# The turn between two expert passes and the last norm: rest rows packed on 128 partitions, the third slab split ahead of the output copies, one of each token's two rows gathered in the last pass, the root by Sqrt

## The chip, the cores and the metric

The kernel runs on one core of one Trainium2 chip. The metric is the device time of one execution in microseconds (us). TensorE (PE in the rows; PEld is its weight load), VectorE (DVE), ScalarE (ACT), GpSimd (POOL) and SyncE (SP) run their own instruction streams and meet at semaphores. Transfers are issued from the queues of SP, ACT and POOL.

## The reference

Two decoder layers over 512 prompt tokens and 8 sample tokens (520 rows of 1024, fp32). Each layer mixes tokens (mLSTM, gated linear attention and pooling in parallel, merged by gates) and then mixes channels: layer 0 by a dense SwiGLU, layer 1 by a mixture of eight experts of which each token uses two. A norm of each row ends the kernel. What matters here:

```python
def moe_swiglu(h, router_w, wg, wu, wd):
    ...
    top_p, top_i = lax.top_k(probs, TOP_K)
    top_p = top_p / jnp.sum(top_p, axis=-1, keepdims=True)
    ...
    for e in range(N_EXPERTS):
        out = out + comb[..., e:e + 1] * swiglu(h, wg[e], wu[e], wd[e]).astype(jnp.float32)
    return out.astype(h.dtype)
...
def rmsnorm(x, g):
    xf = x.astype(jnp.float32)
    y = xf * lax.rsqrt(jnp.mean(xf * xf, axis=-1, keepdims=True) + EPS)
    return (y * g.astype(jnp.float32)).astype(x.dtype)
```

## The kernel before

Every weight tile is a slab of 512 KB (128 partitions of 1024 fp32). SyncE loads it into one of `RAW` = 4 places of `raw`; ScalarE copies it, rounded, to `w_hi` (`split_hi`, L685 in the profile); VectorE (`split_lo`, L1025) or GpSimd (`rest`, L643) writes the remainder to `w_lo`; TensorE multiplies with both. `w_hi` and `w_lo` have `SPL` = 3 places, so a split waits until TensorE is through with the slab three before it (`slab_done`). Which slabs GpSimd takes is fixed by `REST_ON_GPSIMD`: slabs 2 and 3 of a pass and its eleven down slabs.

The experts run in passes. The router sorts the 520 x 2 chosen rows by expert into a DRAM tensor, `token_slots`, `CAP` = 160 slots for a pass; each expert has at least one pass, and in the profiled execution there are eight. A pass has `S_JOB` = 33 slabs: a gate and an up slab for each of `FE_TILES` = 11 hidden tiles, and a down slab for each; the down product of tile f runs after gate and up of tile f + 1. So slabs 0 to 3 are gate, up, gate, up, and slab 4 is the first down. The loop over the passes runs on all five engines.

While pass j multiplies, GpSimd loads the 160 rows of pass j + 1 into `rows_in` (`load_rows`): 128 rows on 128 partitions, and the other `REST` = 32 on 32 partitions. Near the end of pass j TensorE turns these rows, features to partitions, in two halves (`gather`, L1827 for the 128 and L1828 for the 32 rows): the second half of the features after the last up slab, the first half right ahead of the last down. ScalarE and VectorE split each half into `hg` (`gathered_hi`, L918; `gathered_lo`, L1376). The last down also needs `ma_parts` of the last hidden tile, which VectorE completes at L1503, in its order behind the second half of `hg`.

The turn, once the last down is done: ScalarE copies the pass's outputs from PSUM (`yt`, L960, L962), splits slab 2 of the next pass, waits for VectorE to add two partial sums of the 32 rows (L1497), issues the two stores (L966, L967), goes back to the loop's head, reloads the table for Sigmoid (L941), and takes gate tile 0 (L948) and the split of slab 3. The slabs 0 and 1 were split before. GpSimd takes the remainder of slab 2, issues `load_rows` and takes that of slab 3.

After the last pass, GpSimd waits for the stores to land (`all_stored`) and gathers both rows of each token, five tiles of tokens (four of 128, one of 8), into `first` and `second` by indirect DMA (L674), ten transfers in turn. `last_norm` then takes tile by tile: VectorE adds both rows with their shares to `xt` (L1514, L1518), ScalarE squares and sums (L974), takes Ln and Exp for the inverse root (L977, L980) and scales (L983), TensorE turns the tile back (L1956), VectorE multiplies by the gain (L1524), SyncE stores it. VectorE takes the two additions of tile i ahead of the multiplication of tile i - 1.

## Time and profile before

| | us |
|---|---|
| median of three runs | 2482.98 (2480.99 to 2484.28) |
| the profiled execution, its own time | 2478.01 |
| span of its trace | 2476.3 |
| outside the span | 1.7 |

The trace is of a single execution whose time lies 4.97 us under the median of the runs. The passes fill the trace from about 1784 us to 2431 us; the rest behind them is the last norm. In the rows, a start is counted from the first instruction; "xN" counts instructions that are shown as one; what stands in square brackets is how long the engine had been idle, and what released it.

### The profile page before, as it was taken

What the parts mean: (1) busy time and instruction counts of PE and PEld (TensorE: products, weight loads), DVE (VectorE), ACT (ScalarE), POOL (GpSimd) and SP (SyncE); (2) the same over time, 40 slices, a digit from 0 to 9 for tenths busy, and PEclk for the clock granted to TensorE, in tenths of its full rate; (3) what the DMA queues carried; (4) which work ended last, traced back from release to release, by engine and by line L of the source; (5) the groups of instructions that cost most, each with busy time, mean ns of one, the idle gap of its engine ahead of it and who ended that gap; (6) DMA issues with size and microseconds to landing.
All of it is one profiled execution on the core that took longest, in us unless ns stands there. A gap on an engine that the chain in (4) does not pass through costs nothing.

```text
span 2476.3 us, 39023 instructions
## 1 busy us (share of the span) xinstructions
PE 2235.2 (90%) x15763; PEld 2044.0 (83%) x15763; DVE 1227.6 (50%) x1718; ACT 941.7 (38%) x1258; POOL 441.4 (18%) x387
## 2 busy tenths in 40 slices
PE   6999999749899999989999997598699999999994
PEld 6999887539899999989998875398588888887883
DVE  3225433655343332232254336553377777677775
ACT  3224333141333322132244231413355555555556
POOL 0000212131000000000002121310233443444343
PEclk9999999769999999999999997699699999999996
DMA  4323422325523332323234223251377777776775
GB/s 141 93 86 99 148 75 84 111 87 167 228 79 91 93 94 86 92 64 93 86 99 148 79 79 117 86 164 60 123 223 236 225 230 227 235 233 225 236 226 173
DMA packets 102634, 341.70 MB, mean 138 GB/s; under 512 B 13128, under 2 KB 17256, under 8 KB 102248
## 3 DMA queue, kind: packets, MB, share of 16 engines
q1 hardware_dynamic: 85416, 278.46, 36.3%
q0 software_dynamic: 15568, 56.34, 6.8%
q10 hardware_dynamic: 1536, 5.24, 0.6%
q8 instruction: 89, 1.46, 0.2%
q14 instruction: 25, 0.20, 0.0%
HBM read 294.28 MB, written 46.17 MB: 137 GB/s over the span
## 4 chain that ended last, share of the span: by engine, by line
PE 61%; issue 18%; POOL 10%; DVE 5%; ACT 4%; DMA 1%; POOLq 0%; SPq 0%; ACTq 0%; DVEq 0%
PE ps L1574 49%; PE ps L1568 9%; POOL w_lo L643 9%; DVE h_lo L1045 1%; DVE sq L1040 1%; POOL br_lo L612 0%; DMA ifb<-if_bias 0%; POOL token_slots L658 0%; ACT mixed L851 0%; ACT L805 0%; ACT wgt L805 0%; DVE Cs L1262 0%; DVE num L1267 0%; DVE Cq L1264 0%; ACT w_hi L685 0%
## 5 line engine op out<-in xcount | busy, mean ns | idle before, releaser
L685 ACT ACTIVATE w_hi<-raw 128x1024 fp32r<-128x1024 f32 x488 | 514.0, 1055 | 569.3 <-PE ps L1574 492.6
L1025 DVE TENSOR_TENSOR w_lo<-raw,w_hi 128x1024 fp32r<-128x1024 f32 x383 | 473.1, 1235 | 380.9 <-ACT w_hi L685 377.5
L1574 PE MATMUL ps<-h_hi,w_hi 128*128 128x260 f32 x2800 | 587.8, 292 | 34.2 <-DVE h_lo L1045 26.0
L1574 PE MATMUL ps<-h_hi,w_lo 128*128 128x260 f32 x2800 | 573.5, 287 | 0.0
L1574 PE MATMUL ps<-h_lo,w_hi 128*128 128x260 f32 x2800 | 572.9, 287 | 0.0
L1574 PEld LDWEIGHTS ps<-h_hi,w_hi 128*128 128x128 f32 x2800 | 442.4, 193 | 56.1 <-issue 46.9
L1574 PEld LDWEIGHTS ps<-h_hi,w_lo 128*128 128x128 f32 x2800 | 441.5, 193 | 0.0
L1574 PEld LDWEIGHTS ps<-h_lo,w_hi 128*128 128x128 f32 x2800 | 440.9, 193 | 0.0
L1883 PE MATMUL ps<-hg,w_hi 128*128 128x320 f32 x1408 | 378.1, 351 | 27.7 <-POOL w_lo L643 25.4
L1885 PE MATMUL ps<-hg,w_lo 128*128 128x160 f32 x1408 | 337.3, 240 | 0.0
L643 POOL TENSOR_TENSOR w_lo<-raw,w_hi 128x1024 fp32r<-128x1024 f32 x105 | 250.2, 2387 | 397.2 <-ACT w_hi L685 397.0
L1883 PEld LDWEIGHTS ps<-hg,w_hi 128*128 128x128 f32 x1408 | 269.4, 191 | 39.1 <-POOL w_lo L643 28.0
L1885 PEld LDWEIGHTS ps<-hg,w_lo 128*128 128x128 f32 x1408 | 273.9, 195 | 3.2
L1897 PE MATMUL ps<-w_hi,ma_parts 128*128 128x512 f32 x352 | 117.4, 415 | 7.0 <-POOL w_lo L643 6.6
L1574 PE MATMUL ps<-br_hi,w_hi 128*128 128x260 f32 x384 | 81.0, 294 | 45.3 <-issue 35.9
L1482 DVE TENSOR_TENSOR ma<-gsum,msig 128x160 f32<-128x160 f32 x88 | 82.4, 936 | 52.6 <-ACT msig L948 52.6
L1574 PEld LDWEIGHTS ps<-br_hi,w_hi 128*128 128x128 f32 x384 | 62.4, 198 | 46.4 <-issue 36.7
L563 POOL DMA_DIRECT2D S_p<-S x2 | 1.2, 598 | 481.5 <-DVE S L1116 481.5
L1480 DVE TENSOR_REDUCE gsum<-ps 128x160 f32<-128x320 f32 x88 | 43.2, 490 | 85.4 <-PE ps L1885 85.2
L560 POOL DMA_DIRECT2D m_s<-ml_m x2 | 1.1, 552 | 450.3 <-DVE x L1368 450.3
L1574 PE MATMUL ps<-br_lo,w_hi 128*128 128x260 f32 x384 | 80.3, 291 | 0.0
L1574 PE MATMUL ps<-br_hi,w_lo 128*128 128x260 f32 x384 | 79.8, 290 | 0.0
(336 smaller groups left out, 2724.6 us busy)
## 6 DMA issues: line engine op xcount, KB each, us to landing
raw<-slabs SPq DMA_DIRECT2D x489, 512.0 KB, 3.9
gates_kept<-sq SPq DMA_DIRECT2D x64, 260.0 KB, 2.1
gs<-gates_kept POOLq DMA_DIRECT2D x64, 260.0 KB, 3.2
token_slots<-zeros POOLq DMA_DIRECT2D x1, 9600.0 KB, 34.7
rows_in<-token_slots POOLq DMA_DIRECT2D x9, 512.0 KB, 5.6
Cs<-ml_C POOLq DMA_DIRECT2D x8, 512.0 KB, 4.1
C_s<-Cs POOLq DMA_DIRECT2D x8, 512.0 KB, 2.9
token_slots<-yt ACTq DMA_DIRECT2D x8, 512.0 KB, 2.7
```

The costliest lines, as they stand in the source:

```text
L643: nc.gpsimd.tensor_tensor(w_lo[:, n % SPL], raw[:, place(n)], w_hi[:, n % SPL].bitcast(F32), ALU.subtract).then_inc(lo_ready_gpsimd, 1)
L685: nc.scalar.activation(w_hi[:, n % SPL], raw[:, place(n)], ACT.Copy).then_inc(hi_ready, 1)
L1025: tt_op(w_lo[:, n % SPL], raw[:, place(n)], w_hi[:, n % SPL].bitcast(F32), ALU.subtract).then_inc(lo_ready, 1)
L1040: stt_op(to, x[:, kk], gain[:, kk:kk + 1], rs[:, 0], ALU.mult, ALU.mult).then_inc(normed, 1)
L1045: tt_op(h_lo[:, kk - 1], own, h_hi[:, kk - 1].bitcast(F32), ALU.subtract).then_inc(h_lo_ready, 1)
L1480: nc.vector.tensor_reduce(gsum[:], addends(b), AX.X, ALU.add).then_inc(m_sum, 1)
L1482: tt_op(ma[:, f % 2], gsum[:], msig[:], ALU.mult).then_inc(m_gate, 1)
L1568: return mm(out, a, b, start=start, stop=stop, skip_group_check=True)
L1574: ins = mm(out[:, hf], wgt_part[:, slot, tile], in_part[:, kk, HALF * hf:HALF * (hf + 1)], start=first and not ends and in_part is in_hi, ...
L1883: mm(out[:, 0:2 * CAP], w_hi[:, (s0 + s) % SPL, kk], hg[:, kk], start=kk == 0, stop=False, skip_group_check=True)
L1885: ins = mm(out[:, 0:CAP], w_lo[:, (s0 + s) % SPL, kk], hg[:, kk, 0:CAP], start=False, stop=kk == KT - 1, skip_group_check=True)
L1897: mm(ps[:, 4 + hf_], parts[:, at:at + P], w[:, slot_n, 4 * hf_:4 * hf_ + 4], start=f == 0 and a == 0, stop=f == FE_TILES - 1 and a == 2)
```

## The change

Five edits go together.

- The 32 rest rows of a pass are no longer loaded on 32 partitions but as four quarters of their features, one below the other, on 128 partitions (`rest_in`, four transfers instead of one). TensorE turns them with two full transposes, in the second half of the features, in place of eight narrow ones spread over both halves. ScalarE and VectorE split them by an operation of their own.
- In the turn, ScalarE splits slab 2 of the next pass ahead of the two output copies instead of behind them.
- The two slots of a token are sorted (`order`), and the shares with them. The row of the lower slot lies in an earlier pass than that of the higher. GpSimd's last pass is taken out of its loop, and between its remainders it gathers the five tiles of lower rows; after the last pass only the five of higher rows are gathered.
- The inverse root of the last norm is Sqrt on ScalarE and a reciprocal on VectorE instead of Ln and Exp.
- The last norm's order: VectorE adds all lower rows first, then the higher rows tile by tile, with the gain of tile i - 2 behind the addition of tile i; ScalarE squares tile i ahead of scaling tile i - 1.

```diff
@@ GpSimd
         def load_rows(first):
-            pool.dma_start(rows_in[:, 0], slots[bass.ds(first, P)]).then_inc(rows_loaded, 16)
-            pool.dma_start(rows_in[0:REST, 1], slots[bass.ds(first + P, REST)]).then_inc(rows_loaded, 16)
+            pool.dma_start(rows_in[:], slots[bass.ds(first, P)]).then_inc(rows_loaded, 16)
+            for b in range(4):
+                pool.dma_start(rest_in[REST * b:REST * (b + 1)],
+                               slots[bass.ds(first + P, REST), D // 4 * b:D // 4 * (b + 1)]).then_inc(
+                                   rows_loaded, 16)
...
-        with pool.Fori(0, passes_pool) as j:
+        with pool.Fori(0, last) as j:
             pool.wait_ge(gathered, j * 2 + 2)
             load_rows(j * CAP + CAP)
-            for i in REST_ON_GPSIMD[1:] + [S_JOB + 2]:
-                rest(MOE0 + i, j)
+            pass_rests(j, REST_ON_GPSIMD[1:] + [S_JOB + 2])
+        pool.wait_ge(gathered, last * 2 + 2)
+        load_rows(last * CAP + CAP)
+        pass_rests(last, REST_ON_GPSIMD[1:4])
+        pool.wait_ge(y_stored, last * 32 + 1)
+        for i in range(5):
+            rest(MOE0 + REST_ON_GPSIMD[4 + i], last)
+            rows_back(first, 0, i, first_in)
+        pass_rests(last, REST_ON_GPSIMD[9:] + [S_JOB + 2])
         pool.wait_ge(all_stored, 1)
         for i in range(5):
-            rws = slice(0, tile_rows(i))
-            for k, (to, landed) in enumerate(((first, first_in), (second, second_in))):
-                pool.indirect_dma_start(to[rws, i], None, slots,
...
+            rows_back(second, 1, i, second_in)
@@ ScalarE
             nc.scalar.activation(hg_part(b, 0), gathered_ps(b), ACT.Copy).then_inc(hg_hi_ready, 1)
+            if b:
+                nc.scalar.activation(hg_rest(0), gathered_rest(), ACT.Copy).then_inc(hg_hi_ready, 1)
...
             gathered_hi(j + 1, 0)
+            split_hi(s0 + 2, j + 1)
             act.wait_ge(slab_done, j * S_JOB + (s0 + S_JOB))
...
-            split_hi(s0 + 2, j + 1)
             act.wait_ge(y_added, j + 2)
@@ VectorE
             tt_op(hg_part(b, 1), gathered_ps(b), hg_part(b, 0).bitcast(F32),
                   ALU.subtract).then_inc(hg_lo_ready, 1)
+            if b:
+                tt_op(hg_rest(1), gathered_rest(), hg_rest(0).bitcast(F32),
+                      ALU.subtract).then_inc(hg_lo_ready, 1)
...
+            inc(tt_op(order_f[:, 0], index_f[:, 0], index_f[:, 1], ALU.min))
+            inc(tt_op(order_f[:, 1], index_f[:, 0], index_f[:, 1], ALU.max))
...
+            for i in range(7):
                 if i < 5:
...
                     dve.wait_ge(second_in[i], 16)
...
+                if 1 <= i < 6:
+                    rws = slice(0, tile_rows(i - 1))
+                    dve.wait_ge(fin_root, i)
+                    nc.vector.reciprocal(rst[rws, i - 1:i], rst[rws, i - 1:i]).then_inc(fin_rs, 1)
+                if i > 1:
+                    rws = tile_rows(i - 2)
+                    dve.wait_ge(fin_turned, i - 1)
@@ TensorE
         def gather(p, b):
-            pe.wait_ge(rows_loaded, p * 32 + 32)
+            if b:
+                pe.wait_ge(rows_loaded, p * 80 + 80)
+                for c in range(2):
+                    nc.tensor.transpose(ps[:, 2 + c, P:2 * P], rest_in[:, c * P:(c + 1) * P], ident)
             for m in range(4 * b, 4 * b + 4):
-                out = ps[:, m // 2, 256 * (m % 2):256 * (m % 2) + CAP]
-                nc.tensor.transpose(out[:, 0:P], rows_in[:, 0, m * P:(m + 1) * P], ident)
-                ins = nc.tensor.transpose(out[:, P:CAP], rows_in[0:REST, 1, m * P:(m + 1) * P],
-                                          ident[0:REST, 0:REST])
+                ins = nc.tensor.transpose(ps[:, m // 2, 256 * (m % 2):256 * (m % 2) + P],
+                                          rows_in[:, m * P:(m + 1) * P], ident)
```

On ScalarE, at the end of a pass, these rows stand from the split of the first half of `hg` to the stores. First the kernel before:

```order
L918 ACTIVATE hg<-ps 128x4x160 [waits gathered]
L958 REGISTER_ALU
L959 ISA [waits slab_done]
L960 ACTIVATE yt<-ps 128x1024 [waits y_stored]
L962 ACTIVATE yt<-ps 32x1024
L682 ISA
L684 ISA [waits arrived3]
L685 ACTIVATE w_hi<-raw 128x1024 [waits slab_done]
L965 REGISTER_ALU
L966 ISA [waits y_added]
L966 DMA token_slots<-yt 128x1024
```

And the same stretch of ScalarE in the changed kernel, whose line numbers differ (L716 is the split, L994 and L996 the copies):

```order
L949 ACTIVATE hg<-ps 128x4x128 [waits gathered]
L713 ISA
L715 ISA [waits arrived3]
L716 ACTIVATE w_hi<-raw 128x1024 [waits slab_done]
L992 REGISTER_ALU
L993 ISA [waits slab_done]
L994 ACTIVATE yt<-ps 128x1024 [waits y_stored]
L996 ACTIVATE yt<-ps 32x1024
L998 REGISTER_ALU
L999 ISA [waits y_added]
L999 DMA token_slots<-yt 128x1024
```

The split of slab 2 has moved from behind the two copies to ahead of them; the wait for `y_added` still stands behind all three.

On VectorE, near the end of a pass, the changed kernel has these rows between the multiplication of the last hidden tile (L1535) and the remainder of that tile (L1551), which the last down waits for:

```order
L1535 TENSOR_TENSOR ma<-ma,usum 128x160 [waits m_up]
L1057 REGISTER_ALU
L1058 TENSOR_TENSOR w_lo<-raw,w_hi 128x1024 [waits hi_ready]
L1408 ISA
L1409 TENSOR_TENSOR hg<-ps,hg 128x4x128 [waits hg_hi_ready]
L1412 TENSOR_TENSOR hg<-ps,hg 128x2x4x32
L1551 TENSOR_TENSOR ma_parts<-ma,ma_parts 128x128 [waits m_hi]
L1551 TENSOR_TENSOR ma_parts<-ma,ma_parts 128x32
```

Before, one operation of 128x4x160 stood where L1409 and L1412 stand now; the rest is as it was.

On ScalarE the last norm of the changed kernel begins with these rows:

```order
L1044 ACT_TABLE_LOAD
L1044 ACTIVATE msig<-con 1x1 [waits y_stored]
L1008 ACTIVATE rows_in,ssq<-xt 128x1024 [waits both_added]
L1011 ACTIVATE rst<-ssq,con 128x1 [waits fin_sq]
L1008 ACTIVATE rows_in,ssq<-xt 128x1024 [waits both_added]
L1011 ACTIVATE rst<-ssq,con 128x1 [waits fin_sq]
L1016 ACTIVATE xt<-xt,rst 128x1024 [waits fin_rs]
L1008 ACTIVATE rows_in,ssq<-xt 128x1024 [waits both_added]
```

The nine table loads that stood between the Ln and the Exp of the tiles are gone; the one ahead of the wait for the stores is left.

## Rows read from the trace of the kernel before

**Rows 1.** Waits of TensorE over all passes: total us, times, longest.
```profile
PE ps L1883 <- POOL w_lo L643: 25.4, 14, 2.3
```

**Rows 2.** Windows from turn to turn: length, engines' busy us, granted clock, DMA share.
```profile
1945.75:2026.52 80.77, 76.76 (x480) 67.26 (x480) 58.32 (x89) 45.62 (x61) 32.04 (x15) 0.98 0.73 231
2026.52:2107.34 80.82, 75.96 (x480) 65.98 (x480) 58.82 (x89) 45.73 (x61) 32.04 (x15) 1.00 0.74 230
```

**Rows 3.** Timeline of TensorE, first turn: start, us, engine, line, operation.
```profile
1870.12 0.41 PE L1883 MATMUL ps<-hg,w_hi 128*128 128x320 f32 x1 [1.38 <-POOL w_lo L643]
...
1874.74 0.41 PE L1883 MATMUL ps<-hg,w_hi 128*128 128x320 f32 x1 [2.32 <-POOL w_lo L643]
```

**Rows 4.** Timeline of ScalarE, first turn.
```profile
1864.77 1.03 ACT L960 ACTIVATE yt<-ps 128x1024 f32<-128x1024 f32 x1 [1.88 <-PE ps L1901]
1865.69 1.00 ACT L962 ACTIVATE yt<-ps 32x1024 f32<-32x1024 f32 x1
1866.59 1.04 ACT L685 ACTIVATE w_hi<-raw 128x1024 fp32r<-128x1024 f32 x1
...
1869.44 1.28 ACT L941 ACT_TABLE_LOAD   x1 [1.81 <-issue]
...
1871.21 1.04 ACT L685 ACTIVATE w_hi<-raw 128x1024 fp32r<-128x1024 f32 x1
```

**Rows 5.** Timeline of VectorE, first turn.
```profile
1860.63 0.81 DVE L1376 TENSOR_TENSOR hg<-ps,hg 128x640 fp32r<-128x640 f32 x1
1861.37 0.38 DVE L1503 TENSOR_TENSOR ma_parts<-ma,ma_parts 128x128 fp32r<-128x128 f32 x2
...
1866.72 1.21 DVE L1497 TENSOR_TENSOR yt<-yt,ps 32x1024 f32<-32x1024 f32 x1 [2.94 <-ACT yt L962]
```

**Rows 6.** Timeline of GpSimd, first turn: the remainder of slab 3.
```profile
1872.34 2.34 POOL L643 TENSOR_TENSOR w_lo<-raw,w_hi 128x1024 fp32r<-128x1024 f32 x1 [1.25 <-ACT w_hi L685]
```

**Rows 7.** Timeline behind the last pass: gathers, first additions, one tile turned.
```profile
2438.08 1.00 POOL L674 DMA_INDIRECT first<-token_slots,index  x1 [1.68 <-ACT msig L1011]
...
2442.34 1.28 DVE L1514 SCALAR_TENSOR_TENSOR xt<-first,share,xt 128x1024 f32<-128x1024 f32 x1 [8.06 <-DMA first<-token_slots,index]
...
2443.94 1.28 DVE L1518 SCALAR_TENSOR_TENSOR xt<-second,share,xt 128x1024 f32<-128x1024 f32 x1 [0.31 <-DMA second<-token_slots,index]
...
2466.18 1.97 PE L1956 MATMUL ps<-con,xt 128*128 128x128 f32 x8 [3.38 <-ACT xt L983]
```

**Rows 8.** Timeline of TensorE: last transposes ahead of the last down, first turn.
```profile
1861.63 0.33 PE L1827 MATMUL ps<-con,rows_in 128*128 128x128 f32 x1
...
1862.07 0.72 PE L1897 MATMUL ps<-w_hi,ma_parts 128*128 128x512 f32 x2
```

**Rows 9.** Timeline of TensorE in the routing: sixteen full transposes in a row.
```profile
1744.74 1.97 PE L1836 MATMUL ps<-con,hf 128*128 128x128 f32 x16
```

**Rows 10.** Timelines of GpSimd and TensorE ahead of the first pass.
```profile
1772.42 0.57 POOL L650 DMA_DIRECT2D rows_in<-token_slots  x1
...
1777.16 0.45 PE L1827 MATMUL ps<-con,rows_in 128*128 128x128 f32 x1 [9.40 <-DMA rows_in<-token_slots]
...
1784.03 0.63 PE L1883 MATMUL ps<-hg,w_hi 128*128 128x320 f32 x1 [1.65 <-DVE hg L1376]
```

**Rows 11.** Lines of 2431.1 to 2477 us: count, busy us, mean ns, idle before.
```profile
L980 ACT ACT_TABLE_LOAD x5 | 6.4, 1283 | 0.1
...
L983 ACT ACTIVATE xt<-xt,rst 128x1024 f32<-128x1024 f32 (+1 forms) x5 | 5.7, 1147 | 0.2
...
L974 ACT ACTIVATE rows_in<-xt 128x1024 f32<-128x1024 f32 (+1 forms) x5 | 5.3, 1051 | 8.5 <-DVE xt L1518 8.5
L977 ACT ACT_TABLE_LOAD x4 | 5.1, 1283 | 0.1
...
L977 ACT ACTIVATE rst<-ssq,con 128x1 f32<-128x1 f32 (+1 forms) x5 | 1.5, 295 | 0.1
```

**Rows 12.** DMA issues: transfers, KB of each, median us to landing.
```profile
y_out<-x SPq DMA_DIRECT2D x4, 512.0 KB, 3.6
```

More of the change, by code:

```diff
@@ L304, in decoder @@
     xt = sb("xt", [P, 5, D], where=moe)
-    rows_in = sb("rows_in", [P, 2, D], where=moe)
+    rows_in = sb("rows_in", [P, D], where=moe)
+    rest_in = sb("rest_in", [P, D // 4], where=moe)
     yt = sb("yt", [P, 2, D], where=moe)
@@ L322, in decoder @@
     index = sb("index", [P, 2, 5], mybir.dt.int32, where=moe)
+    order_f = sb("order_f", [P, 2, 5], where=moe)
+    order = sb("order", [P, 2, 5], mybir.dt.int32, where=moe)
+    is_low = sb("is_low", [P, 2, 2, 5], where=moe)
     share = sb("share", [P, 2, 5], where=moe)
@@ L663, in _, with pass_rests, rows_back @@
         pool.wait_ge(rt.sem, rt.after("tables"))
-        passes_pool = pool.value_load(jt[:, NJ:NJ + 1], min_val=E, max_val=PASSES)
-        with pool.Fori(0, passes_pool) as j:
+        last = pool.value_load(jt[:, NJ + 1:NJ + 2], min_val=E - 1, max_val=PASSES - 1)
+        def pass_rests(j, which):
+            for i in which:
+                rest(MOE0 + i, j)
+        def rows_back(to, k, i, landed):
+            rws = slice(0, tile_rows(i))
+            pool.indirect_dma_start(to[rws, i], None, slots,
+                                    bass.IndirectOffsetOnAxis(ap=order[rws, k, i:i + 1], axis=0)).then_inc(
+                                        landed[i], 16)
+        with pool.Fori(0, last) as j:
             pool.wait_ge(gathered, j * 2 + 2)
             load_rows(j * CAP + CAP)
-            for i in REST_ON_GPSIMD[1:] + [S_JOB + 2]:
-                rest(MOE0 + i, j)
+            pass_rests(j, REST_ON_GPSIMD[1:] + [S_JOB + 2])
[7 more added lines that the diff above has]
+        pass_rests(last, REST_ON_GPSIMD[9:] + [S_JOB + 2])
         pool.wait_ge(all_stored, 1)
         for i in range(5):
-            rws = slice(0, tile_rows(i))
-            for k, (to, landed) in enumerate(((first, first_in), (second, second_in))):
-                pool.indirect_dma_start(to[rws, i], None, slots,
-                                        bass.IndirectOffsetOnAxis(ap=index[rws, k, i:i + 1], axis=0)).then_inc(
-                                            landed[i], 16)
+            rows_back(second, 1, i, second_in)
     @block.scalar
@@ L1440, in routing @@
             inc(nc.vector.tensor_copy(jt[:, NJ:NJ + 1], ends[0:1, E - 1:E]))
+            inc(ts_op(jt[:, NJ + 1:NJ + 2], ends[0:1, E - 1:E], -1.0, None, ALU.add))
             at("tables")
@@ L1466, in shares @@
             at("share")
+            inc(tt_op(order_f[:, 0], index_f[:, 0], index_f[:, 1], ALU.min))
+            inc(tt_op(order_f[:, 1], index_f[:, 0], index_f[:, 1], ALU.max))
+            for a in range(2):
+                inc(tt_op(is_low[:, 0, a], index_f[:, a], index_f[:, 1 - a], ALU.is_lt))
+                inc(tt_op(is_low[:, 1, a], index_f[:, a], index_f[:, 1 - a], ALU.is_ge))
+            at("masks")
+            inc(nc.vector.tensor_copy(order[:], order_f[:]))
+            inc(tt_op(is_low[:], is_low[:], share[:].unsqueeze(1).to_broadcast([P, 2, 2, 5]), ALU.mult))
+            at("parts")
+            inc(tt_op(share[:], is_low[:, :, 0], is_low[:, :, 1], ALU.add))
+            at("ordered")
         def addends(b):
```

78 lines of the change are left out of this document (40 added, 38 removed).

## The prediction

> **What bounds the kernel now.** I looked first at what TensorE waits for over the passes. One wait stands out: 25.4 us in 14 waits for GpSimd's remainder of a slab [rows 1]; from turn to turn, TensorE is otherwise busy, 76 of some 81 us [rows 2]. The timeline of the first turn shows that these are two waits in each of the seven turns, 1.38 us at slab 2 and 2.32 us at slab 3 [rows 3]; seven times their sum is 25.9, so nearly all of the group is there. The reader is to see that both lie behind ScalarE. Counted from the start of the output copy (1864.77), the second copy starts at 0.92, the split of slab 2 at 1.82, the table load at 4.67 and the split of slab 3 at 6.44 [rows 4]; VectorE's addition of the 32 rows runs from 1.95 to 3.16 [rows 5]; GpSimd takes slab 3's remainder at 7.57 for 2.34 [rows 6], and TensorE goes on at 9.97 [rows 3]. Every step follows on the one before it, and the split of slab 2 lies beside VectorE's addition, for which ScalarE has to wait anyway.
>
> Behind the last pass it is another chain: ten gathers issued one after the other, then five tiles through ScalarE. The gathers start at 2438.08 [rows 7], the span ends at 2476.3, so 38.2 us.
>
> **The third slab ahead of the copies.** In the changed turn, ScalarE splits slab 2 at 0 instead of 1.82, GpSimd takes the remainder from 1.1 to 3.5 (2.34 as in [rows 6]), and TensorE, which came to slab 2 at 3.97 (1870.12 less its wait of 1.38, from 1864.77) [rows 3], does not wait: 1.38 us less. But the copies now start at about 0.95 (a split takes 1.04 and the next operation of a row starts just ahead of its end, as 0.92 behind 1.03 [rows 4]), and VectorE's addition, the stores, the table load and the split of slab 3 all move back by 0.95. Before, the split cost nothing because the addition (1.21) hid it; ahead of the copies nothing hides it. Slab 3 is ready at 10.92 instead of 9.97. TensorE needs slab 3 right behind slab 2, so its 1.38 us are lost again there: it waits once, about 4.7 us, and leaves the turn **0.95 us later**. Bounds: 1.1 (the whole split, 1.04, and the step to the next engine) and 0.8 (if the last down comes 0.15 sooner, below). Seven turns: **+6.7** (5.6 to 7.7). The same 0.95 stands ahead of the stores behind the last pass; I count it there.
>
> **The packed rest rows.** A full transpose and a narrow one take 0.44 between them (1861.63 to 1862.07) [rows 8], eight such pairs a pass 3.5 us. Full transposes in a row take 1.97 / 16 = 0.12 each [rows 9]; ten take 1.2. TensorE has 2.3 us less to do in each pass. What is it worth? In the turn, the last down starts at 1862.07, as soon as the transposes end [rows 8], but VectorE has given it the remainder of the last hidden tile only at 1861.75 (1861.37 and 0.38) [rows 5]: not over 0.3 can be gained. And ahead of that remainder VectorE now has two subtractions of 512 and 256 elements for one of 640; from 0.81 for 640 and 1.21 for 1024 [rows 5] an operation costs about 0.14 and 1.04 ns an element, so the second operation adds some 0.25 with its 128 elements more. I take the two as equal: **0** at the turns, and a new wait of about 2 us ahead of the last down. Bounds: a gain of 0.3 and a loss of 0.25 a pass.
>
> Ahead of the first pass nothing covers the transposes. There the rows landed at 1777.16 and the first product started at 1784.03, 6.87 us later [rows 10]. TensorE runs there at its lower clock (a transpose is 0.45 long, against 0.33 at the turn [rows 8]), where eight full transposes take 1.97 [rows 7], twice what they take in [rows 9], 0.25 each: ten take 2.5 in place of eight pairs. Then the splits set the end: six transposes (1.5) and ScalarE's two copies (about 1.0) put VectorE's three subtractions (0.67, 0.41, 0.67 by the costs above) from 2.5 to 4.3, a gain of 2.6. Against it stand three more issues on GpSimd's queue at 0.59 each [rows 10], 1.8 if the last landing moves by all of it, 0 if it is the 512 KB of the first that end last. The first transfer has most of the bytes, so I take 0.3. **-2.3** (-0.8 to -2.6). In the passes the rows have a whole pass to land, and GpSimd is through with the issues (five at 0.6 behind slab 2's remainder, to about 6.5) before slab 3's split ends at 8.4: 0.
>
> **Lower rows in the last pass.** Five gathers of 512 KB at most, between remainders which take 2.34 and come with every down slab, 80.8 / 11 = 7.3 us apart: GpSimd has room for a 1.0 us issue [rows 7]. Their bytes run beside the slabs' at a DMA share of 0.73 [rows 2]. Gathers alone land 1.60 apart (2442.34 and 2443.94) [rows 7], so each could hold up a slab by 1.6, five 8 us; none if the share that is free takes them. **+0.3** (0 to 8), near nothing, since the free quarter of a 7.3 us step is 1.8. The sorting of slots adds some ten small operations of VectorE while it waits for the first rows anyway.
>
> **The last norm.** Per tile, the Ln, Exp and two table loads become one root: nine loads of 1.283 [rows 11], 11.5 us, go. I follow the new order from the start S of the first of five gathers. Its row tile lands at S + 4.3, the others 1.6 apart [rows 7]. VectorE has added all lower rows by then (five of 1.28 [rows 7], from the end of its last addition on). Tile 1 is added by 7.2, squared (1.05 and the reading of the sum, 1.18 together) and rooted (0.3, as the Ln [rows 11]) by 8.7; tile 0 is scaled (1.15) by 9.9 and turned (1.97 [rows 7]) by 11.9. VectorE stands at the gain of tile 0 until then, and only after it (1.2, as 1024 elements from PSUM in [rows 5]) adds tile 3, by 14.4. So tile 3 is rooted at 15.9, tile 2 scaled by 17.0, turned by 19.1; tile 3 is scaled by 19.8, behind tile 4's root, turned by 21.8, and out of VectorE by 23.0. Its store takes 3.6 [rows 12]: end at S + 26.8, 11.4 less than 38.2. S itself moves by 0.95 against the last down. **-10.4** (-9 to -12, an operation of 1.2 us either way).
>
> **Sum.** -2.3 + 6.7 + 0 + 0.3 - 10.4 = -5.7 us on the profiled execution: 2478.0 to 2472.3. The three runs lie higher, median 2482.98, a factor 1.002, so 2477.3.
>
> **Rivals.** 0.2%, about what a measurement of this kernel can tell from no change, is 5.0 us.
>
> (a) *The split is hidden after all*: slab 3 comes no later, if something other than the chain through the copies held ScalarE's table load. For it speaks that the idle time ahead of that load is put down to issuing [rows 4]; against it that the stores just ahead need VectorE's addition. The turns then cost 0: 2470.6.
>
> (b) *The transposes count*: if the last down could start 2.3 us earlier in eight passes, 18.4 less: 2459. Against it is the remainder of the last hidden tile [rows 5].
>
> (c) *The gathers collide with the slabs* at the full price, 1.6 for each of four large ones, 6.4 more: 2483.4, no change. For it: a slab's load and a gather take the same engines; against: the free share, which is as large as a gather.
>
> (d) *The clock* (slower than before). TensorE's one wait of 4.7 us replaces two of 1.4 and 2.3. After waits the granted clock has fallen: one turn's period shows 0.98 on average, so 0.04 x 80.77 = 3.2 us at the lower level of 1.2 GHz, the next shows 1.00 [rows 2]. If a longer wait brings one such spell more to each turn, TensorE loses half of it, 1.6, seven times 11.4: 2488.7. It decides from 1.5 us lost in a turn, where the gain of 5.7 turns into a loss of 5. The Trainium skill ("TensorE: Matmul & The Clock Gate", "HAM oscillation — how this bites in real kernels") speaks against this change: a wait that is long enough costs the clock, and it should be broken up. The trace agrees that the clock falls after such waits. But it also shows that the period with a spell, 80.77, is no longer than that without one, 80.82 [rows 2], since the slabs behind slab 3 wait for GpSimd anyway; by the rows the price is near 0, by the page's rule 11.4 us.
>
> (e) *Slab 2 still waits*, because its split waits for the same last down as before: it can't start ahead of it. That is so, and is in the sum; if its data had not landed by then it would lose more, but it was split without a wait for data behind the copies [rows 4].
>
> **How the numbers follow.** The sum as it stands has 0.57, and reaches from 2473.5 to 2481.5 for the bounds of the turns, the start and the last norm together; (a) 0.13, (b) 0.06, (c) 0.12, (d) 0.08; 0.04 are left for what I don't see. Under 2478.0 lie somewhat over half of the sum's case (0.33), (a) and (b), and none of the others: faster 0.52. No change: the rest of the sum's case 0.24, most of (c) 0.10, a little of the unseen 0.02: 0.36. Slower: (d), and bits of (c) and the unseen: 0.12. The range 2470 to 2486 leaves out (b), (d) and the unseen; the likeliest case's own is 2473.5 to 2481.5.
>
> **What would show it.** Right: at the turns one wait of TensorE for GpSimd of 4.5 to 5 us at slab 3 and none at slab 2; a new wait of about 2 us for `ma_parts` ahead of the last down; turn to turn 81.8 us instead of 80.8; the first product 2 us sooner; no table load between the tiles; from the first gather behind the last pass to the end some 27 us. Wrong: a period of 80.8 or less (then (a) or (b)), waits for slabs in the last pass that the passes before it lack (c), the lower clock for longer behind each turn and a period over 83 (d), or a last norm that takes over 30 us because a gather lands later than 1.6 behind the one before.

## The result

The changed kernel takes 2486.93 us (median of 12 runs, 2479.20 to 2493.31), the kernel before, run beside it, 2481.34 (12 runs, 2479.64 to 2486.76). The ratio is 1.002, with a 95% interval of 1.0011 to 1.0029: some 5 us slower, where 5.7 us faster was forecast. The profiled execution of the changed kernel took 2483.66, 5.65 more than that of before.

The waits of TensorE over all passes answer to [rows 1] (total us, times, longest):

```profile
PE ps L1938 <- POOL w_lo L655: 32.2, 7, 4.8
PE ps L1952 <- DVE ma_parts L1551: 13.7, 8, 1.7
```

So there are seven waits at slab 3 and none at slab 2, and in each pass a new one of 1.71 us for `ma_parts` ahead of the last down. In the first turn ScalarE does what was forecast, beside [rows 4]:

```profile
1864.00 1.06 ACT L716 ACTIVATE w_hi<-raw 128x1024 fp32r<-128x1024 f32 x1 [2.27 <-PE ps L1956]
1864.97 1.01 ACT L994 ACTIVATE yt<-ps 128x1024 f32<-128x1024 f32 x1
1865.87 0.99 ACT L996 ACTIVATE yt<-ps 32x1024 f32<-32x1024 f32 x1
...
1869.63 1.28 ACT L974 ACT_TABLE_LOAD   x1 [2.76 <-issue]
...
1871.40 1.04 ACT L716 ACTIVATE w_hi<-raw 128x1024 fp32r<-128x1024 f32 x1
```

From the end of the last down (1863.96 here, 1864.65 before) the split of slab 3 starts at 7.44 instead of 6.56. TensorE resumes at 10.96 instead of 10.09 (1874.92 here), 0.87 later, against a forecast of 0.95. The periods, from the end of one last down to the end of the next, are another matter. Their windows, after (length, busy us of PE, PEld, DVE, ACT, POOL, granted clock, DMA share and GB/s), answer to [rows 2]:

```profile
1863.96:1947.33 83.37, 76.11 (x475) 67.51 (x474) 58.51 (x90) 45.86 (x62) 33.53 (x18) 0.96 0.71 224
1947.33:2030.93 83.60, 76.67 (x473) 67.78 (x473) 58.26 (x90) 45.81 (x62) 33.54 (x18) 0.94 0.71 227
...
2280.14:2361.87 81.73, 75.02 (x474) 66.82 (x474) 58.45 (x90) 45.64 (x62) 33.52 (x18) 0.97 0.70 222
2361.87:2445.20 83.33, 76.22 (x473) 67.06 (x471) 58.65 (x90) 45.65 (x62) 38.33 (x23) 0.96 0.75 246
```

One period of seven, 81.73, is the forecast 81.8; the others are 82.8 to 83.6, with the clock at 0.94 to 0.96. All seven sum to 581.2 us against 566.4 before: 14.9 more instead of 6.7. The clock is lost in spells, stretches at half of it. Shorter windows show two of them (same columns), the first over a last down, the second behind a turn:

```profile
2028.20:2031.60 3.40, 3.40 (x11) 2.41 (x10) 0.66 (x2) 0.63 (x1) 0.00 (x0) 0.51 0.93 349
...
1874.60:1881.40 6.80, 6.48 (x22) 5.88 (x23) 5.74 (x8) 2.68 (x4) 2.64 (x2) 0.50 0.53 171
```

Half the clock is the level of 1.2 GHz. Here is the end of the third pass, the first with a spell over its last down: VectorE's subtraction of the second half of `hg`, then TensorE:

```profile
2025.81 0.68 DVE L1409 TENSOR_TENSOR hg<-ps,hg 128x512 fp32r<-128x512 f32 x1
...
2027.18 0.73 PE L1952 MATMUL ps<-w_hi,ma_parts 128*128 128x512 f32 x2 [1.71 <-DVE ma_parts L1551]
2027.75 0.62 PE L1952 MATMUL ps<-w_lo,ma_parts 128*128 128x512 f32 x2
2028.21 1.02 PE L1952 MATMUL ps<-w_hi,ma_parts 128*128 128x512 f32 x2
2029.02 1.06 PE L1956 MATMUL ps<-w_hi,ma_parts 128*64 128x512 f32 x2
2029.88 1.06 PE L1956 MATMUL ps<-w_lo,ma_parts 128*64 128x512 f32 x2
```

From that subtraction to the last down it is 1.37 us, against 1.44 before (1860.63 to 1862.07 in [rows 5] and [rows 8]), so the wait itself makes the last down no later. But about one microsecond behind the wait a pair of products grows from 0.62 to 1.06 us, and this last down takes 3.8 us instead of 2.6 (the four with a spell take 3.8 to 4.1). In the trace of before, five of seven turns have one half-clock spell of 3.41 us, starting 9.9 to 11.6 us behind the last down, and no last down has one. After, four turns have 6.83 us (starting at 8.9 to 10.7), three 3.41, and four last downs have 3.41 us each. Sorted by that, the periods are: 3.41 behind the turn alone, 81.73; 6.83 alone, 82.78 and 83.37; 3.41 and a spell at the last down, 83.11 and 83.33; 6.83 and a spell at the last down, 83.32 and 83.60.

The start, beside [rows 10]: TensorE's first transpose and first product.

```profile
1778.95 0.66 PE L1881 MATMUL ps<-con,rest_in 128*128 128x128 f32 x2 [12.68 <-DMA rest_in<-token_slots]
...
1783.09 0.63 PE L1938 MATMUL ps<-hg,w_hi 128*128 128x320 f32 x1 [1.76 <-DVE hg L1409]
```

The first row transfer was issued at 1773.79, so this is 9.30 us against 12.20 before (1771.82 to 1784.03): 2.9 less. But this execution came to that transfer 1.97 later, in a part of the program that the change leaves as it was.

Behind the last pass, beside [rows 7] and [rows 11]:

```profile
2453.36 1.62 POOL L689 DMA_INDIRECT second<-token_slots,order  x1 [4.65 <-ACT msig L1044]
...
2458.70 1.29 DVE L1568 SCALAR_TENSOR_TENSOR xt<-second,share,xt 128x1024 f32<-128x1024 f32 x1 [3.38 <-DMA second<-token_slots,order]
2460.61 1.28 DVE L1568 SCALAR_TENSOR_TENSOR xt<-second,share,xt 128x1024 f32<-128x1024 f32 x1 [0.62 <-DMA second<-token_slots,order]
```

No table is loaded between the tiles, and from the first gather to the end of the span it is 28.57 us (forecast 26.8); from the last down to the end 36.7, against 45.3 before: 8.6 less.

The two traces differ by 2.0 (ahead of the first transfer) - 2.9 (start) + 0.3 (first pass) + 14.9 (seven periods) - 8.6 (behind the passes) = 5.7.

### The profile page after: what moved, and what is told of

It reads as the page before. It is cut to its first block, busy times and chain, and to the rows that moved or that the text cites. A ratio compares the mean times of both kernels' runs of the same rounds, so it can differ in the third digit from the quotient of the medians.

```text
span 2481.9 us, 39000 instructions
## 1 busy us (share of the span) xinstructions
PE 2226.7 (90%) x15709; PEld 2042.6 (82%) x15709; DVE 1227.9 (49%) x1742; ACT 929.2 (37%) x1253; POOL 454.9 (18%) x414
## 4 chain that ended last, share of the span: by engine, by line
PE 61%; issue 18%; POOL 11%; DVE 5%; ACT 4%; DMA 1%; POOLq 0%; SPq 0%; ACTq 0%; DVEq 0%
PE ps L1628 49%; PE ps L1622 9%; POOL w_lo L655 8%; DVE h_lo L1078 1%; DVE sq L1073 1%; POOL rest_in L663 1%; POOL br_lo L624 0%; PE ps L1938 0%; DMA ifb<-if_bias 0%; PE ps L1952 0%; POOL token_slots L673 0%; ACT w_hi L716 0%; ACT mixed L882 0%; ACT L836 0%; ACT wgt L836 0%
## 5 line engine op out<-in xcount | busy, mean ns | idle before, releaser
L716 ACT ACTIVATE w_hi<-raw 128x1024 fp32r<-128x1024 f32 x488 | 514.6, 1055 | 596.4 <-PE ps L1628 493.4
L1938 PE MATMUL ps<-hg,w_hi 128*128 128x320 f32 x1408 | 384.6, 355 | 34.0 <-POOL w_lo L655 32.2
L1628 PEld LDWEIGHTS ps<-br_hi,w_hi 128*128 128x128 f32 x384 | 62.7, 200 | 45.3 <-issue 36.7
L1952 PEld LDWEIGHTS ps<-w_hi,ma_parts 128*128 128x128 f32 x352 | 61.6, 195 | 34.0 <-DVE ma_parts L1551 15.6
L1628 PE MATMUL ps<-br_lo,w_hi 128*128 128x260 f32 x384 | 80.9, 293 | 0.0
```

The costliest lines, as they stand in the source:

```text
L716: nc.scalar.activation(w_hi[:, n % SPL], raw[:, place(n)], ACT.Copy).then_inc(hi_ready, 1)
L1628: ins = mm(out[:, hf], wgt_part[:, slot, tile], in_part[:, kk, HALF * hf:HALF * (hf + 1)], start=first and not ends and in_part is in_hi, ...
L1938: mm(out[:, 0:2 * CAP], w_hi[:, (s0 + s) % SPL, kk], hg[:, kk], start=kk == 0, stop=False, skip_group_check=True)
L1952: mm(ps[:, 4 + hf_], parts[:, at:at + P], w[:, slot_n, 4 * hf_:4 * hf_ + 4], start=f == 0 and a == 0, stop=f == FE_TILES - 1 and a == 2)
```

## The experiments

Two theories. **The clock**: both waits that the change lengthens or opens, 4.7 us at slab 3 and 1.71 us ahead of the last down, bring longer spells at 1.2 GHz, and these make the passes longer. **The work**: the passes are longer for what runs late in them (slab 3, five row transfers, gathers), and the clock only follows. Each run below was timed in five rounds beside the kernel before; the changed kernel's ratio for comparison is 1.002. Differences between two runs are taken from their ratios.

**Filling the wait ahead of the last down.** The changed kernel, with the four transposes there (of the 128 rows; the rest rows are turned in the other half) done five times over:

```diff
-            for m in range(4 * b, 4 * b + 4):
+            for m in list(range(4 * b, 4 * b + 4)) * (1 if b or isinstance(p, int) else 5):
```

> The changed kernel, but the four transposes of the packed rest rows ahead of the last down are done five times over (same values to the same place), so that TensorE works some 1.75 us where it waited 1.71 us for the packed rows; no result changes. If the wait is what brings the half-clock spell at the last down (four passes of eight in the profile, 1.3 to 1.55 us each): those spells go, the last down takes 2.58 us in every pass, and the time falls by 4 to 6 us against the changed kernel, to 2481 to 2483. If the lower clock only follows from something else, the time stays or rises by up to 8 x 0.1 us, and the spells stay.

2476.53 us, ratio 0.9982 (0.9973 to 0.9991): 0.38% or 9.4 us below the changed kernel, more than expected. One last down, with no wait left ahead of it (the first row is the last ten of twenty transposes):

```profile
2024.33 1.25 PE L1883 MATMUL ps<-con,rows_in 128*128 128x128 f32 x10
2025.55 0.73 PE L1952 MATMUL ps<-w_hi,ma_parts 128*128 128x512 f32 x2
2026.12 0.63 PE L1952 MATMUL ps<-w_lo,ma_parts 128*128 128x512 f32 x2
2026.58 0.62 PE L1952 MATMUL ps<-w_hi,ma_parts 128*128 128x512 f32 x2
```

No last down has a half-clock spell any more. Every turn has one of 6.83 us, and its price depends on where it falls, as this kernel's windows show, the first with a spell from 10.4 us behind the last down, the second from 9.1, the third from 8.1:

```profile
1862.47:1945.64 83.17, 77.69 (x490) 69.20 (x490) 58.44 (x90) 45.86 (x62) 33.53 (x18) 0.96 0.73 225
1945.64:2028.12 82.48, 77.12 (x491) 68.84 (x490) 58.46 (x90) 45.76 (x62) 33.56 (x18) 0.96 0.72 225
...
2274.34:2356.26 81.92, 76.64 (x490) 68.46 (x490) 58.25 (x90) 45.99 (x62) 33.57 (x18) 0.96 0.72 227
```

The earlier the spell begins, the more of it lies in the wait for slab 3 (until 10.9), and the less it costs: from the third window to the first the period grows by 1.25 us. The mean clock of the period, 0.96 in all three, doesn't tell them apart.

**Filling both waits.** As above, and between slabs 2 and 3 forty transposes of a constant:

```diff
+                if f == 1:
+                    for _ in range(40):
+                        nc.tensor.transpose(ps[:, 3, 384:512], ident, ident)
```

> As the run before it, and also forty transposes of a constant between the products of slab 2 and slab 3 of every pass, in place of the wait of 4.3 to 4.8 us at the turn; nothing waits for their output. In the first pass, where there is no such wait, they cost their own 4 to 6 us once. If the clock is the cause: no half-clock spell behind the turn or at the last down, periods of 81.4 to 81.8 us (the period with the fewest spells in the profile has 81.74, which still has one), so 7 x 1.3 = 9 us less, 4 to 6 back in the first pass: 2480 to 2484 in all, with the granted clock up from 0.937. If it is not: periods stay at 83 or rise, and the time rises by the 4 to 6 us of the first pass.

2476.53 us, 0.9978 (0.9969 to 0.9987), less than the 2480 to 2484 expected, but no resolved gain over the one filled wait (0.9982). From the first turn on the clock is at full in every pass, and six periods are 81.4 to 81.6:

```profile
1863.88:1945.51 81.63, 80.11 (x530) 71.19 (x531) 58.90 (x90) 45.54 (x62) 33.63 (x18) 1.00 0.72 228
2353.40:2438.13 84.73, 80.99 (x528) 70.53 (x527) 62.27 (x90) 45.27 (x62) 38.34 (x23) 1.00 0.75 242
```

TensorE takes slab 3 as late as without the transposes (10.99 against 10.95 us behind the last down in the first turn). So, against these 81.6, the run above shows what a spell of 6.83 us costs: 0.3 where it ends 14.9 us behind the last down, 1.6 where it ends at 17.2. Over all runs the mean granted clock is 0.946 here and 0.935 in the changed kernel. The first pass pays for the forty transposes (82.4 us from the first product to its last down instead of 80.5). The last period, 84.73, is a loss of its own, below.

**Slab 2 split behind the copies again.** The changed kernel, ScalarE:

```diff
-            split_hi(s0 + 2, j + 1)
             act.wait_ge(slab_done, j * S_JOB + (s0 + S_JOB))
...
+            split_hi(s0 + 2, j + 1)
             act.wait_ge(y_added, j + 2)
```

> The changed kernel with one edit undone: slab 2 is split behind the output copies again, so the split of slab 3 comes earlier and TensorE waits twice (1.38 and 2.25 us in the trace of before) instead of once for 4.3 to 4.8 us. If the lower granted clock is what made the passes longer than forecast: the seven periods from one last down to the next lose the 0.95 us of the later slab and the second half-clock spell behind the turn (1.0 to 1.6 us, in four of seven turns), and keep the half-clock spell at the last down; so some 82.0 us each instead of 83.0, and 2478 to 2481 us in all, 6 to 9 below the changed kernel. If the passes are longer for work that runs late in them (the later slab alone, five row transfers, packed rows) and the clock follows from that: only 7 x 0.95 = 6.7 us come off if the slab is the cause of nothing else, and the second spell behind the turn stays.

2481.63 us, 0.9995 (0.9984 to 1.0006), 6 us below the changed kernel. But three turns of seven still have 6.83 us at half clock, though their waits are 1.38 and 2.55 us, and two last downs a spell: the one long wait is not needed for it. What came off is about what the later slab costs (6.7 in the forecast), as the second theory had it; for the long wait the clock's theory was wrong.

**That edit of the change alone on the kernel before**, by the two `split_hi(s0 + 2, j + 1)` lines of the change's diff:

> The kernel before with one edit of the change alone: slab 2 is split ahead of the output copies. The additive account of the turn gives 0.95 us later for slab 3 at each of seven turns, 6.7 us in all: 2488. If the longer single wait (4.3 to 4.8 us) also brings a second half-clock spell behind the turn, in four of seven turns at 1.0 to 1.6 us: another 4 to 6 us, 2492 to 2494, and the last down keeps 2.58 us in every pass, since the packed rows are not there. If the second spell comes from the packed rows, it is missing here.

2487.80 us, 1.003 (1.002 to 1.004): 7.4 us, the forecast of 6.7 and no more. Six of seven turns have 6.83 us at half clock, from 7.9 to 8.0 us behind the last down, so that some 3 of them lie in the wait; the periods are 81.7 to 82.1.

**The packed rest rows alone on the kernel before**, by the hunks of `load_rows`, `gather`, `gathered_hi` and `gathered_lo`:

> The kernel before with one part of the change alone: the rest rows packed on 128 partitions (five row transfers, ten transposes, two evictions each way). If the wait of 1.71 us that this opens ahead of the last down costs by the lower clock around it: half-clock spells at the last down in some passes and longer ones behind the turn, as in the changed kernel with the split put back, whose first six periods sum to 492.4 us where before has 485.5; so about 1.1 us in each of seven periods, 8 in all, less up to 1 at the start: 2487 to 2490. If packing costs nothing at the turns, as forecast, and the changed kernel's loss comes of the split moved ahead of the copies: 2480 to 2482.

2486.64 us, 1.0022 (1.0011 to 1.0033): 5.5 us slower, where the forecast has 2.3 faster. Two of its windows:

```profile
1949.42:2030.82 81.40, 74.20 (x475) 64.88 (x474) 59.36 (x90) 45.56 (x62) 33.52 (x18) 1.00 0.72 229
2030.82:2113.24 82.42, 76.30 (x475) 67.46 (x474) 58.77 (x90) 45.81 (x62) 33.47 (x18) 0.96 0.71 225
```

They alternate, four at about 82.45 with a spell of 6.83 us from 9.5 to 9.8 us behind the last down, three at 81.3 to 81.4 with none; the two periods of before that have none are 80.8 and 80.9. So of the 7.5 us by which the seven periods are longer, over half comes with the spells, and some 0.5 us of each period does not. GpSimd at the turn shows most of that:

```profile
2036.19 0.57 POOL L658 DMA_DIRECT2D rows_in<-token_slots  x1
2036.75 1.98 POOL L660 DMA_DIRECT2D rest_in<-token_slots  x4
2038.75 4.68 POOL L652 TENSOR_TENSOR w_lo<-raw,w_hi 128x1024 fp32r<-128x1024 f32 x2
```

The five issues end 7.9 us behind the last down, after slab 3's split (7.5): the remainder starts at 7.93 instead of 7.60, and TensorE resumes at 10.33 instead of 9.99. In the changed kernel this is not so. There the issues end 6.0 us behind the last down, because slab 2 is split early, and slab 3's remainder waits for ScalarE:

```profile
1868.04 1.98 POOL L663 DMA_DIRECT2D rest_in<-token_slots  x4
1872.52 4.71 POOL L655 TENSOR_TENSOR w_lo<-raw,w_hi 128x1024 fp32r<-128x1024 f32 x2 [2.51 <-ACT w_hi L716]
```

No last down of the trace of the packed rows alone has a spell, though the wait of 1.71 us stands ahead of each. Behind its last down this trace is 1.3 us longer than before; no run shows why.

**Packed rows and the filled wait on the kernel before**, the kernel just above with the first diff of this section:

> The kernel before with the packed rest rows alone, and the four transposes ahead of the last down done five times over, so that TensorE works where it would wait 1.71 us. The packed rows alone came to 1.0022 of before (2486.6 us). If their cost is the lower clock that follows that wait: the half-clock spells behind the turns go back to 3.41 us or start early enough to lie in the waits, and what is left is their five row transfers (0.35 us in each turn, from slab 3 resumed at 10.33 instead of 9.99 us behind the last down) less the earlier start: 2480 to 2483. If the cost lies in the transfers, evictions or transposes themselves, filling the wait changes nothing: 2486 to 2488.

2484.92 us, 1.0007 (0.9997 to 1.0017), 3.7 us below the packed rows alone, with intervals that overlap, and between the two expectations. Its profiled execution, at 2488.2 one of its longest, still has 6.83 us behind three turns (82.5 to 82.8); what the fill changed in the others no trace shows.

**The row transfers behind slab 3's remainder**, in the kernel just above:

```diff
+            rest(MOE0 + 3, j)
             load_rows(j * CAP + CAP)
-            for i in REST_ON_GPSIMD[1:] + [S_JOB + 2]:
+            for i in REST_ON_GPSIMD[2:] + [S_JOB + 2]:
```

> The kernel before with packed rest rows and the repeated transposes ahead of the last down, and the five row transfers issued behind GpSimd's remainder of slab 3 instead of ahead of it. Without this move that remainder starts 7.92 us behind the last down and TensorE resumes at 10.33, against 7.60 and 9.99 before. If the three more transfers are what delays it: back to 7.6 and 9.99, periods of 81.05 without a long half-clock spell, 2.4 us less in all than the run without the move (1.0007 of before). If it is not the transfers: 10.33 stays.

2497.64 us, 1.0075 (1.0058 to 1.0091): far slower. TensorE does resume at 10.0, so the 0.34 us were the transfers'. But the issues now hold slab 4:

```profile
2038.50 0.64 PE L1902 MATMUL ps<-hg,w_hi 128*128 128x320 f32 x1 [2.21 <-POOL w_lo L652]
2043.47 1.22 PE L1916 MATMUL ps<-w_hi,ma_parts 128*128 128x512 f32 x2 [0.84 <-POOL w_lo L652]
```

A third wait of 0.8 to 2.7 us follows, spells of up to 10.24 us at half clock, and periods of 82.2 to 84.9.

**What lies behind the passes, alone on the kernel before** (sorted slots, gathers in the last pass, the new order, Sqrt).

> The kernel before with the changes behind the passes alone: the rows of the lower slot gathered in the last pass, the two additions and the scaling in their new order, the root by Sqrt. The turns are those of before, so the periods stay at 80.8 to 81.1 us but for the last, in which the gathers may make the slabs late (ScalarE waits 11.5 to 12.4 us for slabs in the last pass of three runs so far, against 6.2 to 7.9 in a pass without that loss): 0 to 3 us there. The stretch behind the last down falls from 45.3 to 36.7 us. Together 5.5 to 8.6 us below before: 2473 to 2476. If the shorter tail is an effect of the packed rows too, less comes off.

2471.63 us, 0.9966 (0.9953 to 0.9979): 8.4 us faster. All periods are 80.6 to 80.9. From the last down to the end it is 39.2 us, 2.5 more than in the changed kernel; GpSimd and VectorE show why:

```profile
2433.43 7.21 POOL L646 TENSOR_TENSOR w_lo<-raw,w_hi 128x1024 fp32r<-128x1024 f32 x1 [8.17 <-ACT w_hi L704]
2440.80 1.77 POOL L677 DMA_INDIRECT second<-token_slots,order  x1 [0.16 <-issue]
...
2433.58 8.13 DVE L1544 SCALAR_TENSOR_TENSOR xt<-first,share,xt 128x1024 f32<-128x1024 f32 x5
```

The remainder of a next slab that nothing uses lies beside VectorE's five additions and takes 7.21 us instead of 2.34. With the early split it is over before them: the changed kernel with slab 2 split back ends 39.0 us behind its last down, so that edit is worth 2.2 us here in the traces.

**That remainder behind the gathers**, in the kernel just above:

```diff
-        pass_rests(last, REST_ON_GPSIMD[9:] + [S_JOB + 2])
+        pass_rests(last, REST_ON_GPSIMD[9:])
...
             rows_back(second, 1, i, second_in)
+        pass_rests(last, [S_JOB + 2])
```

> The kernel before with the changes behind the passes alone, and one more edit: GpSimd takes the remainder of the next pass's slab 2, which nothing uses behind the last pass, after the gathers of the second slot instead of ahead of them. In the run without it that remainder lies beside VectorE's five additions, takes 7.21 us instead of 2.34, and holds the first gather until 2440.80, 3.6 us behind the stores' landing. If that is what makes this tail 39.2 us where the changed kernel's is 36.7: the tail falls to 35.5 to 36.5, and the time by 2.7 to 3.7 us, to 2468 to 2469. If the gathers are held by the additions in any case: no more than 1 us.

2473.43 us, 0.9966 (0.9952 to 0.9979): no difference in the time. In the trace the gathers start 7.05 us behind the last down instead of 10.4, and the end comes 37.9 us behind it instead of 39.2: 1.3 of the 3.4 arrive. But its last two periods are 82.3 and 82.2 us, where the other five are 80.7 to 80.9.

**The gathers later in the last pass**, in the changed kernel with the one filled wait:

```diff
-        pass_rests(last, REST_ON_GPSIMD[1:4])
+        pass_rests(last, REST_ON_GPSIMD[1:8])
...
-            rest(MOE0 + REST_ON_GPSIMD[4 + i], last)
+            rest(MOE0 + REST_ON_GPSIMD[8 + i], last)
             rows_back(first, 0, i, first_in)
-        pass_rests(last, REST_ON_GPSIMD[9:] + [S_JOB + 2])
+        pass_rests(last, [S_JOB + 2])
```

> The changed kernel with the transposes ahead of the last down repeated, and the five gathers of the lower slot issued behind the splits of the last five down slabs instead of the third to the seventh. In the run without this move the last period is 84.94 us where the one before it is 81.93, and ScalarE waits 12.3 us for slabs there instead of 6.2. If the gathers delay the slabs: the last period falls by 1.5 to 3 us, and the time by as much, to 2473.5 to 2475; if the gathers then land after they are wanted, the tail takes some of that back. If the longer last period has another cause: no difference.

2477.22 us, 0.9993 (0.9984 to 1.0002): no gain. What ScalarE waits for slabs in the last pass, first without the move:

```profile
ACT w_hi L716 <- DMA raw<-slabs: 12.3, 12, 2.5
```

and with it:

```profile
ACT w_hi L716 <- DMA raw<-slabs: 5.5, 6, 1.6
```

The last period falls from 84.94 to 82.53. So the gathers can delay the slabs, by 3 us in that execution and by nothing in the changed kernel's own (7.9 us of waits there, hidden); the timed runs don't confirm a price.

**Both repairs of the turn, in the changed kernel** (slab 2 split back, last wait filled).

> The changed kernel with slab 2 split behind the output copies again, and the transposes ahead of the last down repeated. If both findings add up (6 us from the split, 9 from the filled wait): no half-clock spell at the last down, periods of 81.0 to 81.3 us, some 2470 to 2473. If the filled wait only helps where TensorE waits 4.7 us in one piece at the turn: the periods stay at 82.4 behind the turns with 6.83 us at half clock, and the time is 2476 to 2479.

2475.50 us, 0.9976 (0.9966 to 0.9986). They don't add up: five periods are 81.1 to 81.7, two 82.4 with a spell of 6.83 us. Against the run with slab 2 split back alone (0.9995) the filled wait gives 4.7 us here; the intervals overlap slightly.

**Two attempts at a better turn.** ScalarE splits slab 3 ahead of the table load and slab 4 ahead of the copy of the activation, on the kernel with the last parts alone; and that together with the remainder moved:

```diff
+            split_hi(s0 + 3, j)
             nc.scalar.activation(msig[0:1, 0:1], eps[0:1], ACT.Sigmoid).then_inc(table_loaded, 1)
...
-                if f > 0:
+                if f > 1:
                     split_hi(s0 + gate_slab(f) + 2, j)
...
-                split_hi(s0 + gate_slab(f) + 3, j)
+                split_hi(s0 + gate_slab(f) + (3 if f else 4), j)
```

> The kernel before with the changes behind the passes alone, and another order of ScalarE at the turn: slab 3 is split ahead of the table load instead of behind the first sigmoid, and slab 4 ahead of the copy of the activation. GpSimd can then take slab 3 some 5.9 instead of 7.6 us behind the last down, and TensorE resume at 8.3 instead of 10.0. If the splits bound the turn: 1.7 us in each of seven periods, 12 in all, 2459 to 2461, periods of 79.0. If the activation's remainders on VectorE (4.30 us beside GpSimd's) take over as what the first down waits for: 0.2 us a turn, and 2470.

> Both edits of the two runs before it. They lie in different stretches, so the gains add: 2456 to 2458, if both hold.

2479.31 us, 0.9996 (0.9987 to 1.0005), and 2479.45, 0.9982 (0.9973 to 0.9992), against 0.9966 without. The first is clearly worse; the second looks worse, but its interval overlaps with that of the run without. In the first, TensorE resumes at 9.6 instead of 10.0, and then stands again in five of seven turns:

```profile
2037.31 0.41 PE L1921 MATMUL ps<-hg,w_hi 128*128 128x320 f32 x1 [1.86 <-POOL w_lo L646]
2041.13 0.73 PE L1935 MATMUL ps<-w_hi,ma_parts 128*128 128x512 f32 x2 [1.53 <-DVE ma_parts L1535]
```

The wait for the activation's parts, 1.53, is longer than the 0.4 that the split gained, and the periods are 81.7 to 81.8 instead of 80.7. These five turns have no spell at all, so this loss is not the clock's.

**What pays, put together**: the parts behind the passes, and packed rows for the first pass alone (`is_first`), on each engine as here on GpSimd and TensorE:

```diff
+            if is_first(first):
+                for b in range(4):
+                    pool.dma_start(rest_in[REST * b:REST * (b + 1)],
...
-            pe.wait_ge(rows_loaded, p * 32 + 32)
+            pe.wait_ge(rows_loaded, p * 32 + 80)
+            if is_first(p):
```

> The kernel before with the changes behind the passes, and the rest rows packed for the first pass alone; inside the loop of passes the rows are brought in as before, so the turns and the last down are those of before. From the first row transfer to the first product it is 12.0 to 12.2 us with the old rows and 9.3 to 9.5 with packed ones. If packing costs only at the turns and gains only at the start: 2.6 us less than the changes behind the passes alone (0.9966 of before), so 0.9955 to 0.9958, 2469 to 2471. If the earlier start is lost again on the way to the first last down: 0.9966.

2471.00 us, 0.9953 (0.9939 to 0.9967), the fastest, and faster than both kernels. From the first transfer to the first product it is 9.44 us. Its distance to the parts behind the passes alone, 0.13%, is within the intervals. Its turns have the two waits of before, 1.38 and 2.23 us, and yet the last two have a spell of 6.83 us. The first of these two periods, behind one without a spell:

```profile
2185.19:2265.77 80.58, 75.75 (x481) 66.00 (x480) 58.77 (x89) 45.83 (x61) 32.07 (x15) 1.00 0.71 231
2265.77:2347.96 82.19, 78.11 (x481) 68.69 (x480) 58.18 (x89) 45.87 (x61) 32.06 (x15) 0.96 0.71 228
```

So a long spell behind a turn needs neither of the change's waits.

## Why the prediction was wrong

Measured alone, the parts of the change come to +7.4 (split), +5.5 (packed rows) and -8.4 us (behind the passes): +4.5, and together they were +5.0, which agrees within the intervals (each is 2.5 to 3.2 us to either side). The forecast had +6.7, -2.3 and -10.1. The packed rows can be read a second time, from the changed kernel with slab 2 split back (0.9995) less the parts behind the passes alone (0.9966): +7.2.

- **The third slab ahead of the copies**: right. One wait of 4.3 to 4.8 us, none at slab 2, 0.87 us later at the first turn, and 7.4 us when the edit is made alone.
- **The packed rest rows**: this step failed. "I take the two as equal: **0** at the turns, and a new wait of about 2 us ahead of the last down." The wait came, at 1.71 us, and directly it delays nothing: the last down starts as soon behind VectorE's work as before (1.37 us against 1.44). What was wrong is that I put TensorE's new idle time at nothing since the same operand ended it. Filling that one wait, with the operand no earlier, gave back 9.4 us in the changed kernel; it gave 4.7 with slab 2 split back and 3.7 in the packed rows alone, both with overlapping intervals. In the trace of the packed rows alone the seven periods are 7.5 us longer and the stretch behind them 1.3, against a start that is 2.7 shorter. About 1.1 us comes in each of the four periods that have a spell of 6.83 us; of the 0.5 a period without a spell, 0.34 is the three more issues ahead of slab 3. The forecast of these issues (ended at 6.5, ahead of slab 3's split) held in the changed kernel, where they end at 6.0; only without the early split do they end at 7.9 and cost anything.
- **The clock**, rival (d), at 0.08: "by the rows the price is near 0". That was the reading that failed. The rows [rows 2] compared a turn whose spell of 3.41 us had its cost taken up by slack with one that had none. A spell twice as long, later, or on the last down, costs 1.0 to 1.6 us, and the seven periods came out 8.2 us above the forecast; the sign that I had named, a period over 83, came in five of seven. I had also looked at the wrong wait: made alone, the edit that brings the longer wait at slab 3 cost no more than the later slab, and filling that wait too gained nothing that the runs resolve. The Trainium skill ("TensorE: Matmul & The Clock Gate", "HAM oscillation — how this bites in real kernels") has a rule against long idle gaps of TensorE, because the clock falls after them. These traces agree that waits cost the clock: with both filled it reads 1.00 in the periods, against 0.94 to 0.97. But the page speaks of long gaps, and here the one worth filling was the short one of 1.71 us.
- **The start**: right in mechanism, -2.9 against -2.3 in the traces; as a time it is not resolved.
- **Lower rows in the last pass**: 0 in the changed kernel's trace and in that of the parts behind the passes alone, 3 us in those of the two filled kernels; no clear price in the time.
- **The last norm**: right in mechanism, mis-sized: -8.6 for -10.4. The first gather was issued in 1.62 us instead of 1.00, beside VectorE's additions, and landed 5.34 us behind its start instead of 4.3. (The forecast's own last step, 23.0 and 3.6, makes 26.6 and not 26.8; that changes nothing.)

What stays open: how the 9.4 us of the filled wait are made up. The two profiled executions differ by only 4.2, of which 1.2 lies ahead of the passes, 2.5 in the periods, and a late-slab loss of 3 us in the last pass hides more. Open too is why that wait brought a spell over the last down in four passes of the changed kernel, in two with slab 2 split back, and in none with packed rows alone. That the filled wait pays is shown by the times; that it pays through the clock is shown for the spells over the last downs, which are gone with it, but not for all of the 9.4 us. The spells behind the turns can't all be laid on the change, since the last kernel has two of 6.83 us with the waits of before.

## What to carry to other kernels

A wait that is free because something else ends last is not free if TensorE used to work there: the clock may fall for the work behind it, so price it at both levels, and ask how much slack stands behind it. Before an edit takes work from TensorE ahead of an operand that isn't earlier, see whether the work can stay, or fill the gap with repeats. Measure the parts of a change one at a time: here one of three was worth more than all together.

## What the runs showed of the hardware

- Four issues of 32 KB took GpSimd's queue 1.98 us (0.50 each), where one of the same 128 KB took 0.50.
- Forty transposes of a constant (4.53 us), put in place of a wait of 4.7 us, kept the clock at 1.00 over the turn, where a spell of 6.83 us stood without them.
- A remainder on GpSimd took 7.21 us instead of 2.34 beside five additions of VectorE, which took 8.13 instead of 6.05.
- The part of the program ahead of the passes varies by itself: the first row transfer was issued between 1768.9 and 1776.7 us in these traces. That is as much as the changes under study, and a single trace can't average it out.
